# A two-block network kernel: feed-forward down projection by tokens, up weights cast on ScalarE, loads regrouped

## The reference

```python
def _swiglu(h, w_in, w_out):
    gate, up = jnp.split(h @ w_in, 2, axis=-1)
    return (jax.nn.silu(gate) * up) @ w_out
...
        hin = x * (1 + sc2) + sh2
        y = _swiglu(hin, ffn_w_in[i], ffn_w_out[i])
        x = _layernorm(DEEPNORM_ALPHA * x + (1 + gt2) * y, ln_g[i, 1], ln_b[i, 1])
```

## Time and profile before

| what | value |
|---|---|
| median of 3 runs | 3373.51 us (3361.95 to 3380.45) |
| profiled execution, its own time | 3365.04 us |
| span of that execution | 3363.3 us |
| TensorE busy (matmuls), share of the span | 2770.8 us, 82% |
| VectorE busy | 1986.0 us, 59% |
| ScalarE busy | 839.5 us, 25% |
| mean granted TensorE clock | 0.918 of full speed |
| first feed-forward | 694.6 to about 1189 us |
| second feed-forward | 1586.8 to about 2088 us |

### The profile page before, as it was taken

How to read it: one execution, slowest core, us unless ns; L and a number is a source line. 1 busy time by engine, 2 the same in 40 slices (tenths; PEclk the granted TensorE clock), 3 DMA queues, 4 the chain that set the end, 5 groups by cost and what they waited for, 6 DMA issues and landing times. The chain is left out here.

```text
span 3363.3 us, 40902 instructions
## 1 busy us (share of the span) xinstructions
PE 2770.8 (82%) x16025; PEld 1875.5 (56%) x16025; DVE 1986.0 (59%) x2675; ACT 839.5 (25%) x958; POOL 351.5 (10%) x182
## 2 busy tenths in 40 slices
PE   1899899749999769775899994899985499999991
PEld 0343789337767534442677672444442487777780
DVE  6753455757772418433677534296343488889883
ACT  0301111011110022430111000202200277677762
POOL 0000000210000120002000002000000123333321
PEclk9899899879989889998899896999997699999995
DMA  7221000246642281001555333122024389999962
GB/s 300 91 74 41 7 4 4 114 152 180 180 139 81 81 273 50 1 1 64 156 175 175 107 93 107 68 75 75 25 100 168 126 327 352 344 340 344 336 256 115
DMA packets 237647, 479.29 MB, mean 143 GB/s; under 512 B 33766, under 2 KB 176638, under 8 KB 224217
## 3 DMA queue, kind: packets, MB, share of 16 engines
q1 hardware_dynamic: 213080, 452.01, 38.5%
q0 software_dynamic: 14368, 23.79, 2.1%
q10 hardware_dynamic: 10082, 1.83, 0.3%
HBM read 471.15 MB, written 36.87 MB: 151 GB/s over the span
## 5 line engine op out<-in xcount | busy, mean ns | idle before, releaser
L49 PE MATMUL ffn_bank<-ffn_xT_high,ffn_wi_high 128*128 128x512 f32 x704 | 282.1, 401 | 35.3 <-DVE ffn_xT_low L43 24.3
L50 PE MATMUL ffn_bank<-ffn_xT_low,ffn_wi_high 128*128 128x512 f32 x704 | 276.7, 393 | 0.0
L51 PE MATMUL ffn_bank<-ffn_xT_high,ffn_wi_low 128*128 128x512 f32 x704 | 276.6, 393 | 0.0
L1893 PE MATMUL hyb_bank<-hyb_hT,hyb_wr 128*128 128x512 f32 x512 | 223.6, 596 | 2.0 <-ACT hyb_sga L2021 2.0
L49 PEld LDWEIGHTS ffn_bank<-ffn_xT_high,ffn_wi_high 128*128 128x128 f32 x704 | 133.7, 190 | 82.3 <-DVE ffn_wi_low L43 29.7
L43 DVE TENSOR_TENSOR moe_d_low<-moe_d,exp_d_high 128x4096 fp32r<-128x4096 f32 x32 | 141.6, 4425 | 56.6 <-ACT exp_d_high L2653 56.6
L442 DVE SCALAR_TENSOR_TENSOR ffn_nsum<-ffn_nw,ffn_cond,ffn_nsum 128x256 f32<-128x256 f32 x336 | 163.0, 485 | 12.0
L1893 PEld LDWEIGHTS hyb_bank<-hyb_hT,hyb_wr 128*128 128x128 f32 x512 | 97.2, 191 | 122.9 <-issue 122.9
L43 DVE TENSOR_TENSOR moe_g_low<-moe_g,exp_g_high 128x4096 fp32r<-128x4096 f32 x32 | 141.4, 4419 | 17.3 <-ACT exp_g_high L2653 17.3
L51 PEld LDWEIGHTS ffn_bank<-ffn_xT_high,ffn_wi_low 128*128 128x128 f32 x704 | 133.7, 190 | 28.8
L50 PEld LDWEIGHTS ffn_bank<-ffn_xT_low,ffn_wi_high 128*128 128x128 f32 x704 | 134.0, 190 | 26.8
(11 more groups left out here) (580 smaller groups left out, 5800.9 us busy)
## 6 DMA issues: line engine op xcount, KB each, us to landing
moe_g<-in_w_e_gate SPq DMA_DIRECT2D x32, 2048.0 KB, 8.0
moe_u<-in_w_e_up SPq DMA_DIRECT2D x32, 2048.0 KB, 9.6
moe_d<-in_w_e_down SPq DMA_DIRECT2D x32, 2048.0 KB, 9.4
ffn_wi<-in_ffn_w_in SPq DMA_DIRECT2D x88, 512.0 KB, 5.2
mod_ring<-in_ada_w SPq DMA_DIRECT2D x8, 3072.0 KB, 22.5
ffn_nw<-in_ada_w SPq DMA_DIRECT2D x24, 1024.0 KB
ffn_nw<-in_w_ada SPq DMA_DIRECT2D x24, 1024.0 KB
ffn_wo<-in_ffn_w_out SPq DMA_DIRECT2D x44, 512.0 KB, 3.6
```

What stands on the lines that cost most here:

```text
L49: nc.tensor.matmul(out, w[0], x[0], start=start, stop=False, **kw)
L50: nc.tensor.matmul(out, w[0], x[1], start=False, stop=False, **kw)
L51: return nc.tensor.matmul(out, w[1], x[0], start=False, stop=stop, **kw)
L1893: last = nc.tensor.matmul(bank[job_bank[n]][:, :], lhs, rhs, start=(k == 0), stop=(k == KD - 1))
```

## The change

Five edits, all in `swiglu`, which runs twice.

1. Down projection by tokens. The products are turned round: `act` is the stationary operand, 128 tokens at a time, and 512 columns of `w_out` move. The eight banks then hold four tiles of tokens by two halves of the width, already in the form that `deepnorm_rows` reads. The zero products, the copies to `yT` and the transposes back are gone.
2. The first 18 slices f are done for all four tiles each; the last 4 slices are done tile by tile, so that tile 0 is complete first.
3. `w_out` has a ring of four buffers in place of two, in memory that the up weights have left; the loops over f are written out.
4. The cast to `wi_high` is done by ScalarE (`cast_in`). On VectorE `split_in` keeps only the rest, and it stands in another place: for slice n+2, right behind `gate_up` of slice n.
5. At the start, SyncE issues the load of slice 0 ahead of `x`, TensorE starts on the first chunk of `xT` while VectorE splits the next ones, and the modulation pieces run one step further ahead (two pieces before slice 0, and two per slice in the first pair).

The core of the diff:

```diff
@@ SyncE
+                sp.dma_start(ident[:, :], ident_dram).then_inc(s["ident_loaded"], 16)
+                load_in(0, 0)
+                for t in range(NT):
+                    sp.dma_start(x[:, t, :], x_in[t * P:(t + 1) * P, :]).then_inc(s["x_loaded"], 16)
+                load_in(1, 1)
                 sp.wait_ge(s["xT_psum"], KD)
                 load_piece(0, 0)
-                with sp.Fori(0, PAIRS - 1) as i:
+                load_piece(1, 1)
+                def pair(i):
                     for h in range(2):
-                        sp.wait_ge(s["nsum_done"], i * 2 + h + 1)
-                        load_piece(i * 2 + (h + 1), 1 - h)
+                        if isinstance(i, int):
+                            for b in range(2):
+                                sp.wait_ge(s["nsum_done"], 2 * h + b + 2)
+                                load_piece(2 * h + b + 2, b)
+                        else:
+                            sp.wait_ge(s["nsum_done"], i * 2 + (h + 4))
+                            load_piece(i * 2 + (h + 4), h)
                         sp.wait_ge(s["act_done"], i * 2 + (h + 3))
                         load_in(i * 2 + (h + 2), h)
...
+                for f in range(NF):
+                    slot = f % WO_RING
+                    if f == 0 or f == 2:
+                        sp.wait_ge(s["hidden"], 2 * (NF - 1) + f)
+                        sp.wait_ge(s["wi_split"], NF - 1 + f // 2)
+                    if f >= WO_RING:
+                        sp.wait_ge(s["down_used"], f - WO_RING + 1)
+                    sp.dma_start(wo[slot][:, :], w_out_v[f]).then_inc(wo_loaded[slot], 16)
@@ TensorE
-                for n in range(KD):
-                    nc.tensor.matmul(bank[n][:, :], zero[:, 0:P], zero[:, :], start=True, stop=False, skip_group_check=True)
...
+                def down(f, t):
+                    toks, slot = slice(t * P, (t + 1) * P), f % WO_RING
+                    for j in range(NH2):
+                        cols = slice(j * HALF, (j + 1) * HALF)
+                        last = matmul_halves(nc, bank[2 * t + j][:, :], (act_high[:, f, toks], act_low[:, f, toks]),
+                                             (wo_high[slot][:, cols], wo_low[slot][:, cols]), start=(f == 0), stop=(f == NF - 1))
+                        if f == NF - 1:
+                            last.then_inc(s["y_psum"], 1)
+                    return last
+                for f in range(STEADY):
+                    pe.wait_ge(s["wo_split"], f + 1)
+                    for t in (3, 0, 2, 1):
...
+                        last = down(f, t)
+                    last.then_inc(s["down_used"], 1)
                 for t in range(NT):
-                    for j in range(2):
-                        for n in range(4):
-                            last = nc.tensor.transpose(bank[2 * t + j][:, n * P:(n + 1) * P],
-                                                       yT[:, 4 * j + n, t * P:(t + 1) * P], ident[:, :])
-                        last.then_inc(s["y_psum"], 1)
+                    for f in range(STEADY, NF):
+                        if t == 0:
+                            pe.wait_ge(s["wo_split"], f + 1)
+                        down(f, t)
@@ ScalarE
+                def cast_in(n, h):
+                    act.wait_ge(wi_loaded[h], n // 2 * 32 + 32 if isinstance(n, int) else (n - h) * 16 + 32)
+                    nc.scalar.copy(wi_high[h][:, :, :, :], wi[h][:, :, :, :]).then_inc(s["wi_highs"], 1)
...
+                def pair(i, more):
                     for h in range(2):
                         act.wait_ge(s["hidden"], i * 4 + (2 * h + 1))
                         act.wait_ge(s["act_done"], i * 2 + h + 1)
                         nc.scalar.activation(sil[:, h, :], bank[2 * h][:, :], ACT.Silu).then_inc(s["sil_done"], 1)
+                        if more:
+                            act.wait_ge(s["hidden"], i * 4 + (2 * h + 2))
+                            cast_in(i * 2 + (h + 2), h)
...
@@ VectorE
                 def split_in(n, h):
-                    dve.wait_ge(wi_loaded[h], n // 2 * 32 + 32 if isinstance(n, int) else (n - h) * 16 + 32)
-                    nc.vector.tensor_copy(wi_high[h][:, :, :, :], wi[h][:, :, :, :]).then_inc(s["wi_highs"], 1)
                     dve.wait_ge(s["wi_highs"], n + 1)
                     low_half(nc.vector, wi_low[h][:, :, :, :], wi[h][:, :, :, :], wi_high[h][:, :, :, :]).then_inc(s["wi_split"], 1)
...
-                with dve.Fori(0, PAIRS - 1) as i:
+                def pair(i):
                     for h in range(2):
-                        split_in(i * 2 + (h + 1), 1 - h)
                         gate_up(i * 2 + h, h)
-                        next_piece(i * 2 + (h + 1), 1 - h)
+                        split_in(i * 2 + (h + 2), h)
+                        if isinstance(i, int):
+                            for b in range(2):
+                                dve.wait_ge(s["n_psum"], 2 * h + b + 1)
+                                next_piece(2 * h + b + 2, b)
+                        else:
+                            dve.wait_ge(s["n_psum"], i * 2 + (h + 3))
+                            next_piece(i * 2 + (h + 4), h)
```

More of the change, by code:

```diff
@@ L238, in swiglu @@
         wi_loaded = [room.sem(f"wi_loaded{i}") for i in range(2)]
-        wo_loaded = [room.sem(f"wo_loaded{i}") for i in range(2)]
+        wo_loaded = [room.sem(f"wo_loaded{i}") for i in range(WO_RING)]
         nw_loaded = [room.sem(f"nw_loaded{i}") for i in range(2)]
@@ L277, in _ @@
                         sp.wait_ge(s["act_done"], i * 2 + (h + 3))
                         load_in(i * 2 + (h + 2), h)
[L279 to L287, removed]
+                pair(0)
@@ new lines, in _ @@
+                with sp.Fori(1, PAIRS - 1) as i:
+                    pair(i)
+                for f in range(NF):
[6 more added lines that the diff above has]
+                    sp.dma_start(wo[slot][:, :], w_out_v[f]).then_inc(wo_loaded[slot], 16)
@@ L341, in _ @@
[L341 to L354, removed]
-                for t in range(NT):
-                    for j in range(2):
-                        for n in range(4):
-                            last = nc.tensor.transpose(bank[2 * t + j][:, n * P:(n + 1) * P],
-                                                       yT[:, 4 * j + n, t * P:(t + 1) * P], ident[:, :])
-                        last.then_inc(s["y_psum"], 1)
+                        if isinstance(i, int):
+                            next_sum(2 * h, 0)
+                            next_sum(2 * h + 1, 1)
+                        else:
+                            next_sum(i * 2 + h + 2, h)
@@ new lines, in _ @@
+                pair(0)
+                with pe.Fori(1, PAIRS) as i:
+                    pair(i)
+                def down(f, t):
[7 more added lines that the diff above has]
+                    return last
@@ L383, in _ @@
                         nc.scalar.activation(sil[:, h, :], bank[2 * h][:, :], ACT.Silu).then_inc(s["sil_done"], 1)
-                        next_row(i * 2 + h, h)
-                for p in range(NF, PIECES):
-                    next_row(p, p % 2)
-                for n in range(KD):
-                    act.wait_ge(s["down_done"], n + 1)
-                    nc.scalar.copy(yT[:, n, :], bank[n][:, :]).then_inc(s["yT_done"], 1)
+                        if more:
+                            act.wait_ge(s["hidden"], i * 4 + (2 * h + 2))
+                            cast_in(i * 2 + (h + 2), h)
+                        if isinstance(i, int) and i == 0:
+                            next_row(2 * h, 0)
+                            next_row(2 * h + 1, 1)
+                        else:
+                            next_row(i * 2 + h + 2, h)
+                pair(0, True)
+                with act.Fori(1, PAIRS - 1) as i:
+                    pair(i, True)
+                pair(PAIRS - 1, False)
                 for t in range(NT):
```

84 lines of the change are left out of this document (44 added, 40 removed).

## The result

| | before | changed |
|---|---|---|
| median of 4 runs | 3376.94 us (3361.95 to 3380.45) | 3476.12 us (3467.35 to 3486.30) |
| profiled execution | 3365.04 us | 3473.88 us |
| mean granted TensorE clock | 0.918 | 0.910 |

The ratio is 1.0304, with a 95% interval from 1.0260 to 1.0347: slower, as forecast (3455 us, range 3405 to 3515). The mechanism was the one predicted. Its size was 22 us short, by the profiled executions (87 forecast, 108.8 measured).

The account below looks back on a forecast made before the run. VectorE's ring of load, cast, rest and activation (12.0 us) was taken to bound the up phase, TensorE close behind. Feed-forwards slower by 40.5 and 46.4 us, together 87, took 3365.04 to 3452; forecast 3455 us, range 3405 to 3515.

Parts of the forecast that it names:

- The ring: Up phase: load 6.6, ScalarE cast 1.9, rest 2.21, piece sum 4.44, activation 1.87 in series; 17.0 us per slice against 12.0.
- Rivals 1 to 4: Up-phase alternatives: TensorE-bound 3223 us (0.05); TensorE low-clock 3619 (0.04); 8.3-us loads 3523 (0.09); steps near 15 us 3355 to 3390 (0.03).
- rival 3: Up phase: loads take 8.3 us in each step as modulation and up weights collide; 68 us more, 3523; chance 0.09.
- Rival 1: Up phase: the wait hides and TensorE's 11.5 us set the step; end near 2006, about 3223 us; chance 0.05.
- The start: Start of each feed-forward: transposes begin 5.6 us later; in the second, first activation ends at 1630.0, before 1632.3.
- The steps: Up phase after the first activation: 20 steps of 17.0 us plus two extra piece sums, 8.9, in sum 348.9 us.
- The clock: TensorE, up phase: each slice starts at 1.2 GHz and takes 13.5 us, under 17.0, costing nothing but at the very end.
- The order of the queue: Start: `x` waits behind all of the first slice's 1 MB in ring order, 5.6 us later (bounds 0 and 5.6).
- The down phase: Second feed-forward's down projection: 528 products at 0.227, 119.9 us against 130.0, VectorE waits gone with a ring of four.
- The tail: End of second feed-forward: tile 0 complete 16.3 us before the last product, normalisation 30.6 us, ending at 2120.3.
- gap: Between last up and first down product: the 23.3 us of piece sums and opening zero products go altogether.

Follow-up runs that it names:

- e10: Changed kernel with 17 extra TensorE products behind each slice's row sum from the third on, into an unread bank; 3484.88 us, ratio 1.0331 to before.
- e8: Changed kernel without the tile-by-tile end, all 22 down-phase slices going over all four tiles; 3484.42 us, ratio 1.0321 to before.
- e1: Changed kernel with VectorE's piece sum moved back ahead of the weight rest of slice n+2; 3283.29 us, ratio 0.9737 to before.
- e4: Kernel before with only VectorE's order changed: activation, then cast and rest of slice n+2, then piece sum; 3558.76 us, ratio 1.0541.
- e3: Kernel before with only the changed kernel's down phase, keeping its own start and up phase; 3274.17 us, ratio 0.9719.
- e5: Kernel before with only the cast of the up weights moved to ScalarE; 3413.10 us, ratio 1.0123.

## Why the prediction was right, and where it was short

- The ring. All five members were right, in the mean of the 17 steps: from release to arrival 6.5 us (6.6 taken), cast 1.93 (1.9), rest 2.21 (2.21), piece sum 4.5 (4.44), activation 1.95 (1.87). Rivals 1 to 4 fell: no step was near 12 or 15, TensorE was not bound at the low level, and no load of the plain steps took over 7.2 us, where rival 3 had 8.3 in each. Rival 1's end near 2006 doesn't follow from its own terms, 1630 + 230 + 141.4 = 2001; it decides nothing.
- The start. In the second feed-forward the transposes begin 17.1 us into the stage, against 11.5 before, the 5.6 us forecast (6.3 us later in the first), and the first activation ends 42.8 us into the stage (43.3 forecast).
- The steps. From the first activation to the twenty-first, 353.4 us against 348.9. The 18 plain steps were 0.15 us longer each, 2.7 us. The two with two piece sums took 22.2 and 22.6 us where 17.0 + 4.44 had been taken, 1.9 us more: their loads took 7.4 and 7.7 us beside a piece load issued just ahead of them, not 6.6.
- The clock. Forecast was that each slice starts on the low level, takes 13.5 us and that this costs nothing. The second half holds (e10). The first holds in part: of the 42 slices behind the first of each feed-forward, 12 ran at the full level throughout (11.2 us) and 30 had a low stretch (12.5 to 14.1 us), 8 of them though they started on the full level. The Trainium skill (TensorE: Matmul & The Clock Gate, section "HAM oscillation — how this bites in real kernels") has every tile of its loop begin low, behind a DMA wait of some 3 to 5 us. The trace agrees in the shown pauses of 5.5 and 6.4 us; its 12 full slices stood behind pauses of 1.8 to 3.4 us, most of them shorter than the page's.
- The order of the queue. The Trainium skill (DMA: Bandwidth & Descriptors, section "Queues, rings and completion order") says that each DMA engine consumes the descriptors of one issuer in ring order. By it `x` comes behind the slice issued ahead of it; the trace agrees, with the 5.6 us above.
- The down phase: "a ring of four" was taken to remove every wait. But the last four slices need all four buffers for tile 0 at once, and the load of slice 21 starts only when slice 17 is used. TensorE waits for it, and the phase takes 122.6 us against 119.9 (120.0 in e8, which has no such wait):

```profile
2156.92 0.50 PE L49 MATMUL ffn_bank<-ffn_wo_high,ffn_act_high 128*128 128x512 f32 x1 [2.29 <-DVE ffn_wo_low L43]
```

- The tail. The start of the normalisation was taken from the products alone. `x_again` is queued behind all loads of `w_out`, which was not priced. VectorE waits for it at the start of the normalisation, 14.7 us ahead of the last product and not 16.3, and the end comes 16.1 us behind the last product, not 14.3:

```profile
2160.22 0.69 DVE L532 TENSOR_TENSOR ffn_y<-ffn_bank,ffn_gt 128x512 f32<-128x512 f32 x1 [2.75 <-DMA ffn_x_again<-x]
```

Together, second feed-forward: -0.4 (start) + 4.5 (steps) - 0.3 (gap) + 2.7 (down phase) + 1.8 (tail) = 8.3 us by rounded terms over the 40.5 forecast; from its start to the end of the normalisation it took 541.8 us against 493.1, 48.7 more. In the first it was 540.5 against 486.1, 54.4 more against 46.4. That is 103.1 of the 108.8 us. The other 5.7, less than the 18 us between the runs of one kernel, lie in stages whose code is the same: the attention stage between the two took 413.1 us against 406.1. Its first 100 us, before and after:

```profile
1180.64:1280.64 100.00, 76.00 (x257) 40.77 (x258) 26.88 (x73) 23.58 (x50) 19.56 (x29) 0.87 0.69 224
```
```profile
1236.10:1336.10 100.00, 75.92 (x234) 41.87 (x235) 18.76 (x47) 22.56 (x49) 19.50 (x29) 0.74 0.70 224
```

TensorE is as busy in both and gets fewer products done at the lower clock (0.74 against 0.87). What lowered it wasn't tried.

## What to carry to other kernels

Draw the ring before moving a step: who releases the load, what stands between the release and the use on the same engine, and what of it lies beside the load. Here 4.4 us of independent work cost nothing between the release and the wait, and its full length behind the wait (e1, e4). And a gain at the ends of a stage does not show what the same change did to its 20 steps: start, gap, down phase and tail gave back 62 us per feed-forward (66 forecast) while the steps took 111 and 116; time the parts apart.

## What the runs showed that was not expected

- Where the pause stands ahead of the slice (from the fifth slice on), 12 slices of the changed kernel behind pauses of 1.8 to 3.4 us stayed at the full level and 24 behind pauses of 2.9 to 6.4 us had a low stretch. Yet behind a pause of 2.0 us in the mixer of the kernel before the level was low, and two slices of e10 behind 1.9 and 2.0 us had a low stretch. The pause alone doesn't tell the level.
- A loop of two slices on ScalarE held one ACT_TABLE_LOAD of 1.28 us per round (20 to 22 in before, e3, e4 and e5); with one pair written out ahead of it there were 2. Where silu had room nothing waited for it; where it lay in the ring, writing the pair out gave 12.6 us by the steps of the two traces (17.6 by the medians). Why the load stands in the loop was not tried beyond that.
